# One core of Trainium2: loads reordered in the projections, a third gate buffer in the mixer, the last stage inside the experts' block

## The chip, the cores and the metric

One core of a Trainium2 chip runs one encoder layer in float32. The metric is the device time of one launch in microseconds (us); lower is better. The engines are TensorE (PE, matmuls), VectorE (DVE), ScalarE (ACT), GpSimd (POOL) and SyncE (SP, here only an issuer of DMAs); ACT and POOL issue DMAs as well. Each engine runs its own instructions in order, and waits on semaphores that others raise.

## The reference, cut to what matters

`x` is 512 prompt and 2048 sample tokens of width 1024, in two groups with their own conditioning.

```python
ada = silu(c) @ w_ada + b_ada;  sh1, sc1, gt1, sh2, sc2, gt2 = split(ada, 6)
h = rms_norm(x, norm_pre_mix) * (1 + sc1) + sh1
x = x + gt1 * rms_norm(token_mixer(h), norm_post_mix)
h = rms_norm(x, norm_pre_ffn) * (1 + sc2) + sh2
y = expert_choice_ffn(h)          # 16 experts, each takes its top tokens; y is a scatter-add
out = x + gt2 * rms_norm(y, norm_post_ffn)

# token_mixer: one projection h @ w_in feeds windowed attention and gated linear attention
merged = sigmoid(ga) * (attn @ w_branch_attn) + sigmoid(gg) * (o_g @ w_branch_gla)
return merged @ w_out
```

## The kernel before

Every float32 product is three matmuls of fp32r parts (`product3`, L108 to L112: hi by hi, lo by hi, hi by lo). ACT casts each operand to its hi part and DVE subtracts to get the lo part, so each weight chunk costs ACT a cast and DVE a `tensor_tensor`. The phases run one after the other, each in a block of its own. A block ends with a drain of every engine and a barrier: nothing of the next begins before the slowest engine has drained.

**Projections and attention** (`phase_proj_attn`, L416, about 45 to 845 us of the span). Five blocks of 512 tokens, in each 24 units (`BLOCK_UNITS`, L365), a unit being one 512-column slice of the projection. Block b also makes the normed and transposed `h` of block b+1: its four x tiles are loaded by SP (`load_x`, L529) into two buffers, ACT sums their squares (`squares`, L664) after units 1, 4, 10 and 14, POOL makes the reciprocal root (`rms`), DVE scales (`norm_x`, L809), PE turns the tile (L1022), ACT and DVE evict it, and POOL stores it to `scratch_hT` (`store_h`, L894). A buffer is free for its next x tile when that store has landed (`s_hst`). SP's queue is written by hand: in the loop over chunks c = 3 to 10, `load_w` for chunk c waits for the weight split of an earlier chunk, and tiles 2 and 3 of the block's four are loaded after the weights of c = 7 and c = 9 (L556). ACT begins the phase with nine small DMAs (L685 to L690), then splits the first weights and the first `h`; it ends that opening with a copy of `wa2` that waits for the nine (L694, L695). The gate `la` of the linear attention is read from its PSUM bank by ACT at L644, put through a softplus (L717), and bounded by DVE at L839.

**Gated linear attention** (`phase_gla`, L1100) to about 1541 us.

**The mixer** (`phase_mix`, L1826, about 1541 to 2104 us). Five blocks b of 512 tokens, in each 12 weight chunks m: eight branch chunks (both branch products of 128 channels) and four out chunks. For a branch chunk SP loads the two gate factors (`load_gate`, L1942, 512 KB), ACT takes their sigmoid in place (`gate`, L2029), DVE multiplies both with PE's result (L2126) and adds (L2128), ACT casts the sum to `m_hi` (L2068), and DVE subtracts to `m_lo` (`keep_lo`, L2132). There are two such gate buffers `sg`; the load for chunk m+1 waits until `keep_lo` of chunk m-1 has counted (`s_mlo`). During branch chunks, DVE, ACT, POOL and PE also finish the four token tiles of the block before: rms, gate row, residual x, second rms, PE's turn of the tile and the router's logits (L2288 to L2299, with evictions at L2062 and L2163). In block 0 SP also loads broadcast rows of `ada`, the bias and the norm weights (`load_rows`, at m = 1 for the mixer's gate and at m = 3 for the experts' gate); POOL makes from them two rows of each gate with eight 128x1024 `tensor_tensor` (L2246, L2249). The second pair is stored to `scratch_gate2` at m = 8, which ACT's first eviction of an out chunk waits for (`s_g2`). The last block's four `xn` tiles are stored by POOL (L2239).

**Routing** (`phase_route`, L2356) to about 2178 us, mostly a search for thresholds between DVE and PE.

**Experts** (`phase_experts`, L2575, 2178 to about 3646 us). For each of 16 experts POOL gathers token rows and scatters results; SP streams weights of 1 MB per chunk, ACT casts, DVE subtracts (L2716, L2768), PE multiplies. SP loads the experts' gate rows from `scratch_gate2` during expert 0 (L2660).

**Last stage** (`phase_final`, L2938, in a block of its own). Twenty tiles of 128 tokens: SP loads y (eight buffers), ACT sums squares and issues the stores three tiles behind (L2966, L2971), POOL makes the reciprocal root one tile at a time (L2983, L2985), DVE scales with the gate row and adds x (L2994, L2997) into one of six output buffers. SP waits for the last scatters before the first y load.

Of the kernel before, what the change touches and what calls it, by code (L numbers as in the profile page):

```python
# [8 lines left out]
F32 = mybir.dt.float32  # L9
# [406 lines left out]
def phase_proj_attn(nc, K, I, S):  # L416
# [10 lines left out]
    with Mem(nc, "pa") as M:  # L427
# [94 lines left out]
        with nc.Block() as block:  # L522
            @block.sync
            def _(sp):
# [20 lines left out]
                for b in range(NB):  # L545
# [25 lines left out]
            def _(act):  # L571
# [109 lines left out]

                act.wait_ge(s_z, 1)
# [8 lines left out]
                split_w(0)  # L691
                split_h(0, range(KD))
                split_w(1)
                act.wait_ge(s_c, 144)  # L694
                act.copy(wa2[:], wa_raw).then_inc(s_wa, 1)  # L695
                for b in range(NB):
                    for j, (kind, i, c) in enumerate(BLOCK_UNITS):
# [25 lines left out]
                        if b == NB - 1 and j in ADA:  # L723
                            read_ada(ADA[j])

# [1100 lines left out]
def phase_mix(nc, K, I, S):  # L1826
# [4 lines left out]
    with Mem(nc, "mix") as M:  # L1831
# [25 lines left out]
        s_g, s_sg = [M.sem(f"gate_loaded{i}") for i in range(2)], M.sem("gate")  # L1857
# [8 lines left out]
        s_row, s_add, s_gate, s_g2 = M.sem("rows_spread"), M.sem("gate_biased"), M.sem("gate_made"), M.sem("gate2_stored")  # L1866
# [30 lines left out]
        def x_of(b, t):  # L1897

            if b == LAST and t >= 2:
                return K.h_raw[:, 2 if t == 2 else 0].rearrange("p c n -> p (c n)")  # L1900
            return x[:, t % 2]
# [25 lines left out]
        with nc.Block() as block:  # L1927
            @block.sync
            def _(sp):
# [11 lines left out]
                def load_gate(b, c):  # L1941
                    g = b * KD + c  # L1942
                    if g >= NB * KD:
                        return
                    wait(sp, s_mlo, g - 1)
                    sp.dma_start(sg[:, g % 2], S["gate"][2 * c:2 * c + 2, :, b * BLK:(b + 1) * BLK].rearrange("c p n -> p c n"))\
                        .then_inc(s_g[g % 2], 16)

                def load_x(b, t):
# [3 lines left out]
                    elif t == 3:  # L1953
# [17 lines left out]
                load_gate(0, 1)  # L1971
                sp.dma_start(wr, I["w_router"][0].rearrange("(k p) n -> p k n", p=P)).then_inc(s_c, 16)
                def load_rows(n):
                    gate, beside = (K.gate1, x) if n == 0 else (mix, mix[:, 2:4])
                    at = (2 + 3 * n) * D
                    for g in range(2):
                        sp.dma_start(gate[:, g], S["ada"][g:g + 1, 3 * n * D:(3 * n + 1) * D].broadcast_to([P, D])).then_inc(s_row, 16)
                    sp.dma_start(beside[:, 0], I["b_ada"][:, at:at + D].broadcast_to([P, D])).then_inc(s_row, 16)
                    sp.dma_start(beside[:, 1], I[("norm_post_mix", "norm_post_ffn")[n]].broadcast_to([P, D])).then_inc(s_row, 16)

                for b in range(NB):
                    for m in range(NM):
                        load_w(b * NM + m + 3)
                        if b == 0 and m in (1, 3):
                            load_rows(m // 2)
                        if b == 0 and m == 8:
                            sp.wait_ge(s_gate, 4)
                            sp.dma_start(S["gate2"], mix[:, 0:2].rearrange("p g d -> p (g d)")).then_inc(s_g2, 16)
                        if b and m in (2, 4):
                            load_x(b - 1, (m + 2) // 2)  # L1990
                        if 1 <= m < 7:
                            load_gate(b, m + 1)
# [3 lines left out]
                    load_gate(b + 1, 1)  # L1996
                    load_x(b, 0)
# [3 lines left out]
                for t in range(TPB):  # L2001
                    n = LAST * TPB + t
                    sp.wait_ge(s_x1, n + 1)
                    sp.dma_start(S["x1"][n * P:(n + 1) * P, :], mix[:, t]).then_inc(s_last, 16)

            @block.scalar
            def _(act):
# [17 lines left out]
                def gate(g):  # L2025
                    if g >= NB * KD:
                        return
                    act.wait_ge(s_g[g % 2], 16 * (g // 2 + 1))
                    act.activation(sg[:, g % 2], sg[:, g % 2], ACT.Sigmoid).then_inc(s_sg, 1)  # L2029

                def evict(b, n, t):
                    u = b * NUB + 16 + 4 * n + t
                    act.wait_ge(s_u, u + 1)
                    if n == 0 and t == 0:
                        if b == 0:
                            act.wait_ge(s_g2, 16)
# [27 lines left out]
                def keep_hi(g):  # L2064
# [3 lines left out]
                    act.copy(m_hi[:, g % KD], sg[:, g % 2, 0]).then_inc(s_mhi, 1)  # L2068
# [982 lines left out]
```

## Time and profile before

| what | us |
|---|---|
| median of 3 runs (3712.59 to 3720.0) | 3719.83 |
| profiled execution | 3716.01 |
| its span, first to last instruction | 3714.3 |
| PE busy in the span | 3367.5 (91%) |
| DVE, ACT, POOL busy | 2195.5, 1609.1, 768.3 |
| mean granted TensorE clock | 0.955 of 2.4 GHz |

A row of the profile names the line, the engine, the operation and the operands; after the bar stand busy time, mean duration in ns, and idle time ahead with what ended it. In a table of waits the columns are: engine, line and operand that waited, what released it, then total us, number of waits, and the longest. A window row gives busy us of each engine with its instruction count, the granted clock (1.00 is 2.4 GHz and 0.50 is 1.2 GHz), the mean busy share of the 16 DMA engines, and GB/s.

### The profile page before, as it was taken

The page shows a single profiled execution, that of the slowest core. Times are in us where ns is not written, and L with a number is a line of the kernel's source. Part 1 is how long each engine was busy: PE and PEld are TensorE (multiplying, and loading weights), DVE is VectorE, ACT ScalarE, POOL GpSimd, SP SyncE. Part 2 cuts the span into 40 slices and gives each one's busy share as a digit, 9 for nine tenths or more (in the row PEclk, how much of TensorE's full clock was granted, in tenths as well). Part 3 has the DMA queues.
Part 4 walks back from the last instruction along what each step waited for, and adds up shares of the span by engine and source line. Part 5 has one row for each costly group of instructions (what it writes and reads, how often), then busy time and mean ns, then how long its engine had stood idle before and what let it go on. Part 6 is the DMA issues. An engine that isn't in the chain of part 4 may idle for free. (4 is left out here: it accounts for less than half of the span.)

```text
span 3714.3 us, 58093 instructions
## 1 busy us (share of the span) xinstructions
PE 3367.5 (91%) x21824; PEld 2852.1 (77%) x21824; DVE 2195.5 (59%) x4005; ACT 1609.1 (43%) x2478; POOL 768.3 (21%) x855
## 2 busy tenths in 40 slices
PE   6998999998899999889999549999999999999991
PEld 4777777676677777677777449999999999999991
DVE  3555455554588888555555465655555555555655
ACT  3666565553344444334444214444444444444442
POOL 1111111341134343223333201111111111111106
PEclk8999999998999999989999769999999999999995
DMA  6434344555645454556656325555555555555576
GB/s 218 162 124 147 136 130 148 161 196 162 197 149 167 133 172 130 151 193 224 222 193 218 157 88 183 164 174 174 170 174 164 170 169 168 171 164 173 166 263 240
DMA packets 540148, 637.28 MB, mean 172 GB/s; under 512 B 82528, under 2 KB 420544, under 8 KB 539712
## 3 DMA queue, kind: packets, MB, share of 16 engines
q1 hardware_dynamic: 491184, 485.78, 40.9%
q0 software_dynamic: 41920, 138.48, 11.8%
q10 hardware_dynamic: 6864, 10.60, 0.8%
q8 instruction: 115, 1.88, 0.2%
q14 instruction: 65, 0.53, 0.0%
HBM read 507.86 MB, written 126.91 MB: 171 GB/s over the span
## 5 line engine op out<-in xcount | busy, mean ns | idle before, releaser
L2768 DVE TENSOR_TENSOR moe_w_lo<-c_w_raw,moe_w_hi 128x2048 fp32r<-128x2048 f32 x192 | 439.8, 2291 | 368.6 <-ACT moe_w_hi L2716 368.6
L110 PE MATMUL moe_pg<-c_x_hi,moe_w_hi 128*128 128x320 f32 x2048 | 634.4, 310 | 1.8 <-DVE c_x_lo L2806 1.8
L112 PE MATMUL moe_pg<-c_x_hi,moe_w_lo 128*128 128x320 f32 x2048 | 632.8, 309 | 0.0
L111 PE MATMUL moe_pg<-c_x_lo,moe_w_hi 128*128 128x320 f32 x2048 | 632.8, 309 | 0.0
L2716 ACT CAST moe_w_hi<-c_w_raw 128x2048 fp32r<-128x2048 f32 x192 | 364.1, 1896 | 147.2 <-DMA c_w_raw<-in_w_gate_e_dram 74.2
L110 PEld LDWEIGHTS moe_pg<-c_x_hi,moe_w_hi 128*128 128x128 f32 x2048 | 384.4, 188 | 3.0 <-issue 2.2
L111 PEld LDWEIGHTS moe_pg<-c_x_lo,moe_w_hi 128*128 128x128 f32 x2048 | 384.5, 188 | 0.6
L112 PEld LDWEIGHTS moe_pg<-c_x_hi,moe_w_lo 128*128 128x128 f32 x2048 | 384.4, 188 | 0.0
L110 PE MATMUL gla_pd<-gla_h_hi,gla_w_hi 128*128 128x512 f32 x640 | 261.7, 409 | 26.3 <-DVE gla_h_lo L1228 23.8
L2690 POOL DMA_INDIRECT scratch_y<-moe_ys,moe_isc x48 | 83.1, 1730 | 825.9 <-ACT moe_ys L2757 699.2
L112 PE MATMUL gla_pd<-gla_h_hi,gla_w_lo 128*128 128x512 f32 x640 | 253.2, 396 | 0.0
L111 PE MATMUL gla_pd<-gla_h_lo,gla_w_hi 128*128 128x512 f32 x640 | 252.9, 395 | 0.0
L110 PE MATMUL pa_pu<-pa_h_hi,pa_w_hi 128*128 128x512 f32 x560 | 224.9, 402 | 18.2 <-DVE pa_h_lo L739 18.2
L111 PE MATMUL pa_pu<-pa_h_lo,pa_w_hi 128*128 128x512 f32 x560 | 219.5, 392 | 0.0
L112 PE MATMUL pa_pu<-pa_h_hi,pa_w_lo 128*128 128x512 f32 x560 | 219.4, 392 | 0.0
L1212 DVE TENSOR_TENSOR gla_w_lo<-c_w_raw,gla_w_hi 128x1024 fp32r<-128x1024 f32 x80 | 158.5, 1982 | 85.1 <-ACT gla_w_hi L1206 85.0
L110 PE MATMUL moe_pd<-moe_w_hi,moe_h_hi 128*128 128x512 f32 x512 | 204.4, 399 | 4.0 <-DVE moe_w_lo L2768 4.0
L111 PE MATMUL moe_pd<-moe_w_lo,moe_h_hi 128*128 128x512 f32 x512 | 199.9, 390 | 0.0
L112 PE MATMUL moe_pd<-moe_w_hi,moe_h_lo 128*128 128x512 f32 x512 | 199.8, 390 | 0.0
L2746 ACT CAST moe_h_hi<-moe_hd 128x320 fp32r<-128x320 f32 x128 | 58.9, 460 | 312.6 <-DVE moe_hd L2834 312.6
L110 PEld LDWEIGHTS gla_pd<-gla_h_hi,gla_w_hi 128*128 128x128 f32 x640 | 122.8, 192 | 56.3 <-DVE gla_w_lo L1212 18.8
L732 DVE TENSOR_TENSOR pa_w_lo<-c_w_raw,pa_w_hi 128x2048 fp32r<-128x2048 f32 x45 | 105.6, 2346 | 98.6 <-ACT pa_w_hi L577 98.5
(381 smaller groups left out, 7469.6 us busy)
## 6 DMA issues: line engine op xcount, KB each, us to landing
c_w_raw<-in_w_gate_e_dram SPq DMA_DIRECT2D x64, 1024.0 KB, 4.8
c_w_raw<-in_w_up_e_dram SPq DMA_DIRECT2D x64, 1024.0 KB, 4.8
c_w_raw<-in_w_down_e_dram SPq DMA_DIRECT2D x64, 1024.0 KB, 5.0
c_w_raw<-in_w_in_dram SPq DMA_DIRECT2D x80, 512.0 KB, 3.9
c_w_raw<-in_w_in_dram SPq DMA_DIRECT2D x35, 1024.0 KB
scratch_gate<-gla_sg POOLq DMA_DIRECT2D x80, 256.0 KB, 2.4
mix_sg<-scratch_gate SPq DMA_DIRECT2D x40, 512.0 KB, 5.6
c_h_raw<-scratch_hT SPq DMA_DIRECT2D x37, 512.0 KB, 6.6
```

Of the source, the lines that this page charges most:

```text
L110: pe.matmul(out, w_hi, x_hi, start=start, stop=False)
L111: pe.matmul(out, w_hi, x_lo, start=False, stop=False)
L112: return pe.matmul(out, w_lo, x_hi, start=False, stop=stop)
L732: dve.tensor_tensor(low, w_raw[:, m % 2, :, 0:n], w_hi[:, m % 2, :, 0:n].bitcast(F32), ALU.subtract).then_inc(s_wlo, 1)
L1212: dve.tensor_tensor(w_lo[:, n % WB], w_raw[:, n % 2], w_hi[:, n % WB].bitcast(F32), ALU.subtract).then_inc(d_wlo, 1)
L2690: pool.indirect_dma_start(out=S["y"], out_offset=bass.IndirectOffsetOnAxis(ap=isc[0:ROWS[r], r:r + 1], axis=0), in_=ys[0:ROWS[r], r], in_o ...
L2716: act.copy(w_hi[:, m % 2], w_raw[:, m % 2]).then_inc(s_whi, 1)
L2746: act.copy(h_hi[:, m // 2 * 2 + i, 0:CAP], hd[:, i]).then_inc(s_hhi, 1)
L2768: dve.tensor_tensor(w_lo[:, m % 2], w_raw[:, m % 2], w_hi[:, m % 2].bitcast(F32), ALU.subtract).then_inc(s_wlo, 1)
```

## The change

- Projections: ACT splits the first weights and `h` ahead of the nine small DMAs; the `wa2` copy with its wait is moved behind unit 1 of block 0. On SP's queue x tiles 2 and 3 of a block are loaded after the weights of c = 5 and 7 instead of 7 and 9.
- Mixer: three gate buffers, and the load for chunk m+2 instead of m+1 is issued at the same place; the residual x tiles take one buffer of their own and one in `K.h_raw[:, 2]`. Rows for the mixer's gate are loaded at m = 8 of block 0; the experts' gate is no longer made here, nor stored.
- The last block's four `xn` stores go from POOL to the end of SP's queue, with a semaphore of their own that POOL's first gather waits for.
- Experts: during expert 0 SP loads four broadcast rows (512 KB each) into `gate1` and two tiles of `K.x1`, and POOL makes the experts' gate with four `tensor_tensor` behind its first scatter.
- Last stage: moved to the end of the experts' block. y tiles lie in `w_hi` and `w_lo`, output tiles in `w_raw` and `ys`. POOL's reciprocal roots are made in seven batches. ACT issues stores six tiles behind.

```diff
-                        if c in (7, 9) and b < NB - 1:
-                            load_x(4 * b + (c - 3) // 2)
+                        if c in (5, 7) and b < NB - 1:
+                            load_x(4 * b + (c - 1) // 2)
...
+                split_w(0)
+                split_h(0, range(KD))
                 act.wait_ge(s_z, 1)
                 for n in range(3):
...
-                split_w(0)
-                split_h(0, range(KD))
                 split_w(1)
-                act.wait_ge(s_c, 144)
-                act.copy(wa2[:], wa_raw).then_inc(s_wa, 1)
...
+                        if b == 0 and j == 1:
+                            act.wait_ge(s_c, 144)
+                            act.copy(wa2[:], wa_raw).then_inc(s_wa, 1)
...
-        sg = M.sb("sg", [P, 2, 2, BLK])
+        sg = M.sb("sg", [P, 3, 2, BLK])
-        x = M.sb("x", [P, 2, D])
+        x = M.sb("x", [P, D])
...
-                    wait(sp, s_mlo, g - 1)
-                    sp.dma_start(sg[:, g % 2], ...)
+                    wait(sp, s_mlo, g - 2)
+                    sp.dma_start(sg[:, g % 3], ...)
...
-                        if b == 0 and m in (1, 3):
-                            load_rows(m // 2)
                         if b == 0 and m == 8:
-                            sp.wait_ge(s_gate, 4)
-                            sp.dma_start(S["gate2"], mix[:, 0:2].rearrange("p g d -> p (g d)")).then_inc(s_g2, 16)
+                            load_rows()
...
-                        if 1 <= m < 7:
-                            load_gate(b, m + 1)
+                        if 1 <= m < 6:
+                            load_gate(b, m + 2)
...
+                for t in range(TPB):
+                    n = LAST * TPB + t
+                    sp.wait_ge(s_xn, n + 1)
+                    sp.dma_start(S["xn"][n * P:(n + 1) * P, :], xn_of(LAST, t)).then_inc(K.last_xn_stored, 16)
...
-                for t in range(TPB):
-                    store_xn(LAST, t)
...
-                        sp.dma_start(K.gate1[:].rearrange("p g d -> p (g d)"), S["gate2"]).then_inc(K.s_gate2, 16)
+                        for g in range(2):
+                            sp.dma_start(K.gate1[:, g], S["ada"][g:g + 1, 3 * D:4 * D].broadcast_to([P, D])).then_inc(s_rows, 16)
+                        sp.dma_start(K.x1[:, 0], I["b_ada"][:, 5 * D:6 * D].broadcast_to([P, D])).then_inc(s_rows, 16)
+                        sp.dma_start(K.x1[:, 1], I["norm_post_ffn"].broadcast_to([P, D])).then_inc(s_rows, 16)
...
+                    if is_exp(e, 0):
+                        pool.wait_ge(s_rows, 64)
+                        for g in range(2):
+                            pool.tensor_tensor(K.gate1[:, g], K.gate1[:, g], K.x1[:, 0], ALU.add).then_inc(s_gadd, 1)
+                        for g in range(2):
+                            pool.wait_ge(s_gadd, g + 1)
+                            pool.tensor_tensor(K.gate1[:, g], K.gate1[:, g], K.x1[:, 1], ALU.mult).then_inc(s_gate2, 1)
                 peeled(pool, N_EXP, body)
+                for i, (a, z) in enumerate(BATCHES):   # (0,1) (1,2) (2,4) (4,8) (8,12) (12,16) (16,20)
+                    pool.wait_ge(s_q, z)
+                    pool.tensor_scalar(rs_fin[:, a:z], ss[:, a:z], 1.0 / D, EPS, ALU.mult, ALU.add).then_inc(s_v, 1)
+                    pool.wait_ge(s_v, i + 1)
+                    pool.tensor_tensor(rs_fin[:, a:z], rs_fin[:, a:z], K.neghalf[:, 0:z - a], ALU.pow).then_inc(s_r, 1)
...
+                    act.activation(junk_tile(n), y_tile(n), ACT.Square, accum_out=ss[:, n:n + 1]).then_inc(s_q, 1)
+                    if n >= 6:
+                        store(n - 6)
```

## Rows read from the trace of the kernel before

**Rows 1.** Waits of PE: engine, line, releaser, then total us, times, longest.

```profile
PE pa_pu L1022 <- DVE pa_st L839: 24.8, 4, 7.2
PE pa_pu L110 <- DVE pa_h_lo L739: 18.2, 5, 11.6
PE mix_p_r L2288 <- DVE c_logit L2159: 18.2, 8, 3.5
PE mix_p_r L2299 <- DVE mix_xT L2163: 9.9, 1, 9.9
PE mix_pu L110 <- DVE mix_w_lo L2112: 3.7, 1, 3.7
```

**Rows 2.** Waits of ACT, the same columns.

```profile
ACT mix_sg L2029 <- DMA mix_sg<-scratch_gate: 120.6, 30, 8.8
ACT pa_row L664 <- DMA pa_x<-in_x_sample_dram: 31.2, 4, 8.7
```

**Rows 3.** Windows: us from the span's start, length, busy by engine, clock, DMA.

```profile
136.70:143.50 6.80, 5.16 (x23) 4.76 (x24) 4.75 (x15) 6.74 (x10) 1.53 (x3) 0.50 0.11 41
...
594.10:600.90 6.80, 4.90 (x21) 4.50 (x22) 4.53 (x14) 6.74 (x10) 1.72 (x4) 0.50 0.09 39
...
1597.60:1614.70 17.10, 9.21 (x30) 7.98 (x31) 13.99 (x13) 5.26 (x7) 7.19 (x3) 0.50 0.53 184
...
1666.00:1725.00 59.00, 52.28 (x280) 42.16 (x279) 42.03 (x48) 29.23 (x39) 27.75 (x26) 0.97 0.72 241
...
1976.00:2036.00 60.00, 54.80 (x283) 43.94 (x282) 42.65 (x49) 29.23 (x39) 28.44 (x26) 0.94 0.74 250
...
1550.00:1563.00 13.00, 9.89 (x34) 7.41 (x35) 5.30 (x5) 7.11 (x7) 0.00 (x0) 0.88 0.90 255
3652.00:3690.00 38.00, 0.00 (x0) 0.00 (x0) 32.26 (x26) 16.78 (x30) 34.72 (x26) 0.50 1.01 399
...
3646.50:3714.30 67.80, 0.00 (x0) 0.00 (x0) 50.17 (x40) 22.99 (x40) 53.06 (x40) 0.50 0.79 310
```

**Rows 4.** Timeline of ACT, 127 to 138 us: start, duration, instruction, idle ahead.

```profile
134.94 0.63 ACT L664 ACTIVATE pa_row<-pa_x 128x512 bf16<-128x512 f32 x1 [7.49 <-DMA pa_x<-in_x_sample_dram]
```

**Rows 5.** Timeline of SP's queue, 84 to 132 us: start, duration to the last issue.

```profile
96.04 7.81 SPq L150 DMA_DIRECT2D c_w_raw<-in_w_in_dram  x2
...
129.03 0.56 SPq L531 DMA_DIRECT2D pa_x<-in_x_sample_dram  x1
```

**Rows 6.** Timeline of POOL, 76 to 105 us: the store of an h tile.

```profile
83.33 1.13 POOL L894 DMA_DIRECT2D scratch_hT<-pa_x  x1 [0.54 <-ACT pa_x L672]
```

**Rows 7.** Timeline of ACT, 44 to 64 us: first weight cast of the projections.

```profile
49.86 1.90 ACT L577 CAST pa_w_hi<-c_w_raw 128x2048 fp32r<-128x2048 f32 x1 [6.71 <-issue]
```

**Rows 8.** Timeline of DVE, 1573 to 1606 us: the same operation twice.

```profile
1579.38 3.35 DVE L2112 TENSOR_TENSOR mix_w_lo<-c_w_raw,mix_w_hi 128x1024 fp32r<-128x1024 f32 x1
...
1587.16 1.23 DVE L2112 TENSOR_TENSOR mix_w_lo<-mix_w_third,mix_w_hi 128x1024 fp32r<-128x1024 f32 x1 [0.25 <-ACT mix_w_hi L2017]
```

**Rows 9.** Timeline of POOL, 1573 to 1606 us: the last two of eight gate operations.

```profile
1598.71 6.08 POOL L2249 TENSOR_TENSOR mix_mix<-mix_mix 128x1024 f32<-128x1024 f32 x2
```

**Rows 10.** Timeline of ACT, 1690 to 1705 us: sigmoid of one branch chunk.

```profile
1702.91 1.06 ACT L2029 ACTIVATE mix_sg<-mix_sg 128x1024 f32<-128x1024 f32 x1 [3.88 <-DMA mix_sg<-scratch_gate]
```

**Rows 11.** Drain of POOL at the end of the mixer: count, ns min/median/max, first and last start.

```profile
L1927 POOLq DRAIN  x1: 4447/4447/4447, 2099.3 to 2099.3; - x1
```

**Rows 12.** Drain of POOL at the end of the experts, same columns.

```profile
L2623 POOLq DRAIN  x1: 9573/9573/9573, 3636.8 to 3636.8; - x1
```

**Rows 13.** Groups by line, 3646 to 3714 us: busy us, mean ns, idle before.

```profile
L2985 POOL TENSOR_TENSOR fin_r<-fin_r,c_neghalf 128x1 f32<-128x1 f32 x20 | 29.7, 1484 | 1.7
L2994 DVE SCALAR_TENSOR_TENSOR fin_o<-fin_y,fin_r,c_gate 128x1024 f32<-128x1024 f32 x20 | 25.7, 1284 | 24.8 <-POOL fin_r L2985 24.8
L2983 POOL TENSOR_SCALAR fin_r<-fin_ss 128x1 f32<-128x1 f32 x20 | 23.4, 1169 | 15.4 <-ACT fin_junk L2971 14.0
```

**Rows 14.** Timeline of DVE, 2290 to 2300 us: a weight split of the experts.

```profile
2294.47 2.29 DVE L2768 TENSOR_TENSOR moe_w_lo<-c_w_raw,moe_w_hi 128x2048 fp32r<-128x2048 f32 x1 [2.91 <-ACT moe_w_hi L2716]
```

More of the change, by code:

```diff
@@ L1856, in phase_mix @@
         s_w, s_whi, s_wlo = K.mix_w + [M.sem("w_loaded2")], M.sem("w_hi"), M.sem("w_lo")
-        s_g, s_sg = [M.sem(f"gate_loaded{i}") for i in range(2)], M.sem("gate")
+        s_g, s_sg = [M.sem(f"gate_loaded{i}") for i in range(3)], M.sem("gate")
         s_half, s_u, s_ra, s_rd = M.sem("half_done"), M.sem("unit_done"), M.sem("unit_read_act"), M.sem("unit_read_dve")
@@ L1996, in _ @@
                     load_gate(b + 1, 1)
+                    load_gate(b + 1, 2)
                     load_x(b, 0)
@@ L2067, in keep_hi @@
                         wait(act, s_u, g // KD * NUB)
-                    act.copy(m_hi[:, g % KD], sg[:, g % 2, 0]).then_inc(s_mhi, 1)
+                    act.copy(m_hi[:, g % KD], sg[:, g % 3, 0]).then_inc(s_mhi, 1)
                 split(0)
@@ L2241, in _ @@
                 clear_spent(pool, K)
[L2242 to L2249 removed]
+                pool.wait_ge(s_row, 64)
+                for g in range(2):
+                    pool.tensor_tensor(K.gate1[:, g], K.gate1[:, g], x[:], ALU.add).then_inc(s_add, 1)
+                for g in range(2):
+                    pool.wait_ge(s_add, g + 1)
+                    pool.tensor_tensor(K.gate1[:, g], K.gate1[:, g], K.h_raw[:, 2].rearrange("p c n -> p (c n)"), ALU.mult)\
+                        .then_inc(s_gate, 1)
                 for b in range(LAST):
@@ L2607, in phase_experts, with tile_of, y_tile, o_tile @@
         s_rest = M.sem("unused_rows_zero")
+        s_rows, s_gadd, s_gate2 = M.sem("gate2_rows"), M.sem("gate2_biased"), M.sem("gate2_made")
+        NY, NO = 8, 6
+        NP = N_PROMPT // P
+        ORDER = list(range(NP, NT)) + list(range(NP))
+        BATCHES = [(0, 1), (1, 2), (2, 4), (4, 8), (8, 12), (12, 16), (16, 20)]
+        ss, rs_fin = M.sb("ss", [P, NT]), M.sb("rs_fin", [P, NT])
+        s_st = [M.sem(f"stored{i}") for i in range(NO)]
+        s_q, s_v, s_r, s_m, s_o = M.sem("squares"), M.sem("mean"), M.sem("rstd"), M.sem("normed"), M.sem("made")
+        s_y = [M.sem(f"y_loaded{i}") for i in range(NY)]
+        def tile_of(buffers, i):
+            flat = buffers[i // 4].rearrange("p a n -> p (a n)")
+            return flat[:, i % 4 * D:(i % 4 + 1) * D]
+        def y_tile(n):
+            return tile_of((w_hi[:].bitcast(F32), w_lo[:].bitcast(F32)), n % NY)
+        def o_tile(n):
+            i = n % NO
+            return K.w_raw[:, i // 2, i % 2 * D:(i % 2 + 1) * D] if i < 4 else ys[:, i - 4]
+        def junk_tile(n):
+            return oh[:, n % 4 * 4:n % 4 * 4 + 4].rearrange("p t n -> p (t n)")
         s_yl, s_yp = M.sem("prompt_low"), M.sem("prompt_sum")
@@ L2762, in _, with store @@
                 peeled(act, N_EXP, body)
+                def store(n):
+                    t = ORDER[n]
+                    dst = outs[0][0, t * P:(t + 1) * P, :] if t < NP else outs[1][0, (t - NP) * P:(t - NP + 1) * P, :]
+                    act.wait_ge(s_o, n + 1)
+                    act.dma_start(dst, o_tile(n)).then_inc(s_st[n % NO], 16)
+                for n in range(NT):
+                    act.wait_ge(s_y[n % NY], 16 * (n // NY + 1))
+                    wait(act, s_q, n - 3)
+                    act.activation(junk_tile(n), y_tile(n), ACT.Square, accum_out=ss[:, n:n + 1]).then_inc(s_q, 1)
+                    if n >= 6:
+                        store(n - 6)
+                for n in range(NT - 6, NT):
+                    store(n)
+                for i in range(NO):
+                    act.wait_ge(s_st[i], 16 * len(range(i, NT, NO)))
             @block.vector
@@ L2856, in _ @@
                 peeled(dve, N_EXP, body)
+                dve.wait_ge(s_gate2, 2)
+                dve.wait_ge(K.s_x1, 16 * NT)
+                for n, t in enumerate(ORDER):
+                    dve.wait_ge(s_r, [i for i, (a, z) in enumerate(BATCHES) if a <= n < z][0] + 1)
+                    wait(dve, s_st[n % NO], 16 * (n // NO))
+                    dve.scalar_tensor_tensor(out=o_tile(n), in0=y_tile(n), scalar=rs_fin[:, n:n + 1],
+                                             in1=K.gate1[:, 0 if t < NP else 1], op0=ALU.mult, op1=ALU.mult).then_inc(s_m, 1)
+                    dve.wait_ge(s_m, n + 1)
+                    dve.tensor_tensor(o_tile(n), o_tile(n), kept_x1(K, t), ALU.add).then_inc(s_o, 1)
             @block.tensor
```

123 lines of the change are left out of this document (34 added, 89 removed).

## The prediction

> **What bounds the kernel now.** I read first the busy shares (PE works 91% of the span), then the waits of PE: what the change can win is PE's idle time, the stretches behind it in which PE runs at 1.2 instead of 2.4 GHz, and the last stage, where PE has nothing to do. The experts, 40% of the span, keep PE fed, so nothing is to be had there. The reader should see in PE's waits [rows 1] four turns of x tiles in the projections (24.8 us in all), one opening wait (11.6), the logits in the mixer (18.2 in one of its lines) and two single waits of 9.9 and 3.7 in the mixer's first block; in ACT's waits [rows 2] the same things from the other side: 31.2 us for x tiles, 120.6 for gate factors. The windows [rows 3] show what a stretch is limited by: a turn's stretch at clock 0.50, a branch stage of the mixer with PE busy 52 of 59 us and no engine full, a last stage without PE. Timelines then tell who was late.
>
> **Projections, x tiles.** ACT sits 7.49 us at the squares of x tile 3 and starts them at 134.94 [rows 4]; that load was issued at 129.03 [rows 5], because on SP's queue it stands behind two weight loads that wait for buffers. Behind the squares stands ACT's read of a gate bank, then DVE's L839, then PE's turn. The same four times: 31.2 us for ACT [rows 2], 24.8 for PE [rows 1]. The change puts both x loads one buffer turn earlier. Tile 3 then goes out about where tile 2 does now, 25 us earlier than today, against 5.9 us that its landing took: the wait goes. Cover: the store that frees the buffer is issued at 83.33 [rows 6] and by my estimate takes about what the x load took, 5.9 us; tile 2's load can thus go at 89, while the next weight load goes at 96.04 [rows 5], so SP has 7 us in hand. Next late is ACT's own work: the squares take two halves of 0.63, so the gate bank is read when PE arrives, or up to 1 us after. Behind each gap PE ran at 0.50; first and last of the four stretches show 5.16 and 4.90 us of matmuls [rows 3], so four of them hold some 20, and 10 come back at full clock. Together 24.8 + 10 = 35 at best; without the clock 25. I take 33.
>
> **Projections, opening.** Nine DMA issues stand ahead of the first cast at 49.86, with 6.71 us of idle by "issue" [rows 7]. In front of them the casts start some 4 us earlier, under an 11.6 us wait of PE [rows 1]. But the nine now stand ahead of the second weight split, so the second chunk comes hardly earlier, and the first turn still waits for tables. Between 0 and 4, I take 1.7. The `wa2` copy is one small operation, behind unit 1 no later needed than before, and the nine transfers have landed by then: nothing.
>
> **Mixer, first block.** POOL's last two gate operations run from 1598.71 for 6.08 us [rows 9], and beside such ones DVE's L2112 took 3.35 us, against 1.23 alone [rows 8]. PE waits 3.7 for it and 9.9 for an eviction queued behind it [rows 1], and runs 9.21 us of matmuls at 0.50 [rows 3]. At m = 8 the row loads and the four remaining operations lie in the out stage, where DVE has no weight deadline as close (PE's out chunk has twice the matmuls). 3.7 + 9.9 + 9.2/2 = 18; without the clock 13.6. I take 18. DVE's first gate scaling comes in the next block, a stage later.
>
> **Mixer, blocks 1 to 4.** A gate load is issued when `keep_lo` of the chunk before last has counted, and ACT's sigmoid waits 3.88 us for it [rows 10], thirty times, 120.6 us [rows 2]. It sets DVE's cycle, and behind DVE stand the logits (18.2 us of PE [rows 1]). With a third buffer the load has a whole chunk (59/8 = 7.4 us) more, and the sigmoid finds its data. Then DVE (42 us of 59) and PE (52.3) remain [rows 3]: PE sets the stage. The four windows are 59 to 60 us with PE busy 52.28 in the first and 54.80 in the last [rows 3], so 6.7 and 5.2 us of idle, some 25 in all, and clocks of 0.97 and 0.94 that hold back some 5 more: 30 at best. Some idle stays, since PE has to turn tiles between logits that DVE feeds. Low end 8: as much as if only the clock dips and a few waits went. I take 22, nearer to the idle that the rows show.
>
> **xn stores.** POOL's drain lasts 4.45 us behind its last store [rows 11], and the other engines had finished; SP's queue issues the stores instead. I take 4 (0 to 4.4: at nothing if SP's drain waits as POOL's does). The Trainium skill, "DMA: Bandwidth & Descriptors", section "Issuing engines are not separate DMA queues", says that DMAs of any issuer run on the same 16 engines and that spreading saves only issue time; by that the stores take as long and the sum would be 4 less. The row is about the issuer's drain, on which the page says nothing.
>
> **Last stage.** POOL's drain begins at 3636.8 and takes 9.57 us [rows 12], so the first y load goes at 3646.5; without a block's end it goes when the scatters have landed, 4 to 5.5 us earlier by estimate. Then POOL's pair, 1.48 + 1.17 = 2.65 a tile [rows 13] with its handoffs, paces DVE, whose own two operations fill 50.2 of 67.8 us [rows 3]. Seven batches take POOL off the chain: up to 8 us. Next late are the transfers: share 1.01 at 399 GB/s in the thick of it, mean 0.79 over 67.8 us, which is 53.6 us of full share [rows 3]. So the stage can't shrink below some 56, and the gain is 14 at most. A batch of four also waits for its last tile. 4 if only the start is won. I take 10. The same page, section "Where 436 GB/s comes from", has some 358 GB/s as what HBM gives a core; 20 loads and 20 stores of 512 KB, 21 MB, would be an estimated 59 us, and the gain some 7. The trace has 399 over 38 us, against it.
>
> **Experts' gate, the cost.** Four 512 KB loads take the place of one of 1 MB, and four 128x1024 operations run on POOL beside DVE, 11 us by [rows 9]. DVE's 2.29 us split at 2294.47 [rows 14] is stretched as in [rows 8], 3.35/1.23 = 2.7 times, by 3.9 us. PE's next chunk needs it at once, and a clock that falls would be on top. Between 0 (POOL's operations fall between DVE's) and 6 (two splits in part); I take 3, nearer to one split's stretch. SP's new wait for the gate stands in the last expert, more than a millisecond behind: nothing.
>
> **Sum.** 33 + 1.7 + 18 + 22 + 4 + 10 − 3 = 86; against the profiled 3716 us, 3630. That execution lies 4 below the median of the three, within their spread.
>
> **Rivals.**
> (a) Transfers bound the mixer's branch stage. It moves 241 GB/s at a share of 0.72; a stretch with the same narrow packets shows 255 at 0.90 [rows 3], so some 283 at full share, and 14.2 MB in 50 us: just below the 52 of PE. For it: the loads then crowd. Against: it needs all of PE's idle gone. Mixer gain 8, time 3644.
> (b) The clock stays: PE still pauses a little at each turn, and the halves (10 + 4.6 us) don't come back: 3645. For it: the clock fell after gaps smaller than these too (0.97 and 0.94 in the branch stages). Against: the stretches lie right behind the long waits.
> (c) The last stage stays bound by transfers or the batches' waits: gain 4, 3636; by the page's 358 GB/s 7, 3633.
> (d) The xn stores' landing is waited for on SP as on POOL, which is where the page's rule would lead: 3634.
> (e) The change doesn't do what it says: ACT still waits for x tiles, because the earlier load waits for the h store behind which POOL is late. 33 lost, 3663.
> (f) The other side: SP's queue is in order. If the h store of tile 0 lands after 96 us [rows 5, 6], the weight loads behind the x load come late, and PE with them. It decides from 7 us of lateness; each us beyond costs about one in each of four blocks. To eat 86 us it must be some 22 us beyond, 29 late; at 25 beyond, 3716 + 14 = 3730. The store's issue is fixed by ACT's and DVE's evictions, so this needs a queue that I misread.
>
> **Chances.** Forecast, 3618 to 3641, with (c) and (d) inside it by size: 0.66 (0.06 of it (c) by its own reasons, 0.02 the page's 358, 0.03 (d)). Better than 3618: 0.08. (a) 0.10, (b) 0.08, (e) 0.05, (f) 0.03. Range: 3610 takes the upper ends of all terms (35 + 4 + 18 + 30 + 4.4 + 14, no cost: 105); 3650 holds (a) or (b) with a few us lost elsewhere; it leaves out (e), (f) and (a) with (b). A measurement of this kernel tells 0.2%, 7.4 us, from no change; every case but (f) is beyond it. Faster 0.95, same 0.02, slower 0.03.
>
> **What would show it.** Right: no PE wait at L1022 and no clock of 0.50 behind the four turns; the first mixer block without the 9.9 us wait, its branch stage some 18 us shorter; branch stages of 53 to 55 us with ACT's gate wait near nothing; no 4 us POOL drain before routing; y loads from about 3642 less the rest, and DVE back to back. Wrong: ACT's gate wait remains (a), PE's idle gone but 0.50 still there (b), DVE pausing every fourth tile at the end (c), a new wait of SP at the x loads with PE idle for weights (f), a wait of PE in the second expert over 6 us.

## The result

The changed kernel takes 3629.86 us, median of four runs (3627.0 to 3631.08), the kernel before 3718.02 us (now four runs, 3712.59 to 3720.0); the ratio is 0.9764, interval 0.9747 to 0.9781. The profiled execution has a span of 3629.0 us at a mean clock of 0.964. The forecast was 3630.0. The total hits, but errors of opposite sign cancel in it, as the terms below show.

TensorE runs the same 21824 matmuls in the same order in both kernels, so the start of one and the same matmul can be compared in the two traces. The gain grows and shrinks like this:

| the same point of the work | before, us | after, us | difference | this step | forecast of the step |
|---|---|---|---|---|---|
| first turn of an x tile | 79.15 | 76.73 | -2.4 | opening -2.4 | -1.7 |
| projections, behind the fourth late turn | 700.36 | 661.62 | -38.7 | x tiles -36.3 | -33 |
| mixer, before the gate rows of before | 1559.27 | 1521.36 | -37.9 | +0.8 | 0 |
| mixer, behind them | 1615.57 | 1557.69 | -57.9 | first block -20.0 | -18 |
| mixer, last turns | 2089.15 | 2008.42 | -80.7 | blocks 1 to 4 -22.9 | -22 |
| routing, first product | 2109.26 | 2024.31 | -85.0 | xn stores -4.2 | -4 |
| second expert, before its second chunk | 2295.29 | 2211.94 | -83.3 | +1.6 | 0 |
| a chunk later | 2304.09 | 2232.38 | -71.7 | experts' gate +11.6 | +3 |
| last matmul | 3633.71 | 3562.08 | -71.6 | 0 | 0 |
| end of the span | 3714.3 | 3629.0 | -85.3 | last stage -13.7 | -10 |

The page of the kernel after shows PE's share and its clock in 40 slices: the low slices, in the routing (2019 to 2092 us) and in the last stage, are what is left.

```profile
PE 3349.1 (92%) x21824; PEld 2839.7 (78%) x21824; DVE 2200.8 (61%) x4005; ACT 1608.5 (44%) x2478; POOL 734.5 (20%) x825
...
PEclk9999999999999999999999589999999999999996
```

PE's waits of the kernel after (line, releaser, total us, times, longest), to be held against [rows 1]:

```profile
PE pa_pu L110 <- DVE pa_h_lo L740: 13.6, 5, 6.6
...
PE moe_pg L110 <- DVE moe_w_lo L2831: 8.9, 1, 8.9
...
PE mix_p_r L2287 <- DVE c_logit L2161: 7.1, 9, 1.5
...
PE pa_pu L1023 <- DVE pa_x L803: 1.3, 1, 1.3
```

The four turns (24.8 us) have no row any longer, the logits went from 18.2 to 7.1 us, the single waits of 9.9 and 3.7 us are gone. A row is new: PE waited 8.9 us once for a weight split of DVE in the experts. ACT's rows for x tiles and for gate factors [rows 2] are both gone.

Windows of the kernel after, columns as in [rows 3]: the branch stages that answer to 1666 and 1976 us of before, a stretch behind a turn, the first block's branch stage, the stretch behind the new wait, and the thick of the last stage.

```profile
1608.00:1660.60 52.60, 50.57 (x278) 40.87 (x276) 40.84 (x46) 29.18 (x39) 26.84 (x24) 1.00 0.77 259
1900.70:1954.10 53.40, 51.03 (x282) 41.33 (x281) 41.50 (x47) 29.18 (x39) 27.56 (x25) 1.00 0.78 266
128.00:134.80 6.80, 6.80 (x58) 6.56 (x57) 4.99 (x15) 6.67 (x12) 0.79 (x1) 1.00 0.49 175
1521.40:1557.70 36.30, 36.30 (x177) 30.52 (x176) 27.29 (x39) 19.10 (x22) 0.00 (x0) 1.00 0.79 240
2222.70:2226.80 4.10, 4.06 (x15) 4.06 (x16) 4.10 (x12) 0.00 (x0) 0.01 (x1) 0.50 0.73 251
3571.00:3610.00 39.00, 0.00 (x0) 0.00 (x0) 32.99 (x28) 21.39 (x37) 13.91 (x12) 0.50 1.02 410
```

Behind a turn PE is now busy all of 6.8 us at full clock, where it had 5.16 us at 0.50. The branch stages take 52.6 and 53.4 us instead of 59 and 60, with PE busy 96%. The new wait, like the old ones, is followed by a stretch at 0.50.

Where the new wait comes from stands in the timelines of DVE and POOL from 2205 to 2235 us of the kernel after (start, duration, instruction; L2742 and L2745 are the experts' gate).

```profile
2211.12 11.57 DVE L2831 TENSOR_TENSOR moe_w_lo<-c_w_raw,moe_w_hi 128x2048 fp32r<-128x2048 f32 x1 [2.91 <-ACT moe_w_hi L2762]
...
2224.37 2.28 DVE L2831 TENSOR_TENSOR moe_w_lo<-c_w_raw,moe_w_hi 128x2048 fp32r<-128x2048 f32 x1
```

```profile
2210.71 5.24 POOL L2742 TENSOR_TENSOR c_gate<-c_gate,c_x 128x1024 f32<-128x1024 f32 x2
2215.41 5.12 POOL L2745 TENSOR_TENSOR c_gate<-c_gate,c_x 128x1024 f32<-128x1024 f32 x2
```

DVE's split takes 11.57 us where [rows 14] has 2.29: it was issued 0.4 us behind POOL's first operation and ends 2.2 us behind POOL's last. It wasn't slowed, it stood still for all four.

The last stage by line (busy us, mean ns, idle ahead) and POOL's drain at the end of the mixer, for [rows 13] and [rows 11]:

```profile
L2751 POOL TENSOR_TENSOR moe_rs_fin<-moe_rs_fin,c_neghalf 128x4 f32<-128x4 f32 (+2 forms) x7 | 11.5, 1644 | 0.6
L2925 DVE SCALAR_TENSOR_TENSOR c_w_raw<-moe_w_hi,moe_rs_fin,c_gate 128x1024 f32<-128x1024 f32 x8 | 10.2, 1280 | 12.7 <-POOL moe_rs_fin L2751 12.7
```

```profile
L1929 POOLq DRAIN  x1: 3279/3279/3279, 2012.4 to 2012.4; - x1
...
L1929 SPq DRAIN  x1: 122/122/122, 2018.7 to 2018.7; - x1
```

POOL's seven batches no longer hold DVE: of 12.7 us of idle 11.6 lie ahead of the first tile. POOL's drain now begins at 2012.4, under the mixer's last work, and SP's takes 0.12 us. SP's first y load stands 7.4 us behind the last matmul (3569.5 against 3562.1), where it stood 12.9 us behind it.

### The profile page after: what moved, and what is told of

It reads as the page before. It is cut to its first block and busy times, and to the rows that moved or that the text cites. A ratio compares the mean times of both kernels' runs of the same rounds, so it can differ in the third digit from the quotient of the medians.

```text
span 3629.0 us, 58054 instructions
## 1 busy us (share of the span) xinstructions
PE 3349.1 (92%) x21824; PEld 2839.7 (78%) x21824; DVE 2200.8 (61%) x4005; ACT 1608.5 (44%) x2478; POOL 734.5 (20%) x825
## 5 line engine op out<-in xcount | busy, mean ns | idle before, releaser
L2831 DVE TENSOR_TENSOR moe_w_lo<-c_w_raw,moe_w_hi 128x2048 fp32r<-128x2048 f32 x192 | 449.0, 2339 | 369.1 <-ACT moe_w_hi L2762 369.1
```

Source lines behind the costliest of these rows:

```text
L2831: dve.tensor_tensor(w_lo[:, m % 2], w_raw[:, m % 2], w_hi[:, m % 2].bitcast(F32), ALU.subtract).then_inc(s_wlo, 1)
```

## The experiments

Theory: each term is what its step said, and the new wait is POOL's gate operations shutting DVE out. Each run below changes the changed kernel in one thing, unless it says otherwise. All but one are single executions, to be read against 3627 to 3631 us; the kernel before, run beside them on three occasions, took 3717.85 (seven runs, 3712.51 to 3731.46), 3721.73 and 3718.27 us, so a total alone can be some us off. Sizes therefore come from the start of the same matmul in the two traces, which drifts by 1 to 6 us over the projections and the linear attention without a cause here.

**No gate operations.** The four operations are taken out of POOL's body.

```diff
-                            pool.tensor_tensor(K.gate1[:, g], K.gate1[:, g], K.x1[:, 0], ALU.add).then_inc(s_gadd, 1)
...
-                            pool.tensor_tensor(K.gate1[:, g], K.gate1[:, g], K.x1[:, 1], ALU.mult).then_inc(s_gate2, 1)
...
```

> The changed kernel without POOL's four gate operations in the experts; the row loads and the waits stay, so the experts' gate factor is raw and the output is left incomplete in that. Theory 1 (POOL's operations shut DVE out of its weight split): DVE's split at that place takes 2.3 instead of 11.57 us, PE's 8.9 us wait there goes, the clock stays at 2.4 GHz, and the time falls by some 12 us, to about 3618. Theory 2 (the 2 MB of row loads delay the weights): the wait stays, 3630.

3618.5 us. DVE's split takes 2.29 us, PE has no wait there, and PE gains 11.6 us there on the kernel after. The row loads cost nothing: theory 2 falls.

**One gate operation.**

```diff
-                        for g in range(2):
-                            pool.tensor_tensor(K.gate1[:, g], K.gate1[:, g], K.x1[:, 0], ALU.add).then_inc(s_gadd, 1)
+                        pool.tensor_tensor(K.gate1[:, 0], K.gate1[:, 0], K.x1[:, 0], ALU.add).then_inc(s_gadd, 1)
...
```

> Only the first of POOL's four gate operations is left in the experts (the other three are left out, so the gate is incomplete). If one operation of POOL holds DVE's split up until it ends, the split takes some 2.3 + 2.0 = 4.3 us, PE waits about 1.7 us, and the cost is 2 to 3 us: 3620. If the 11.57 us were a slower rate of DVE beside POOL (2.7 times, as the first block of the mixer before suggests), the split takes some 4 us too, but its end then doesn't follow POOL's end. If the long split has another cause than POOL's operations, it stays at 11.6 us, and the time at 3630.

3620.87 us. DVE and POOL in its timeline:

```profile
2210.53 4.68 DVE L2827 TENSOR_TENSOR moe_w_lo<-c_w_raw,moe_w_hi 128x2048 fp32r<-128x2048 f32 x1 [2.91 <-ACT moe_w_hi L2758]
```

```profile
2210.12 2.93 POOL L2741 TENSOR_TENSOR c_gate<-c_gate,c_x 128x1024 f32<-128x1024 f32 x1
```

4.68 - 2.29 = 2.4 us of standing still, and PE waits 2.0. This is the size that the prediction had counted for all four.

**Sixteen small gate operations.**

```diff
-                            pool.tensor_tensor(K.gate1[:, g], K.gate1[:, g], K.x1[:, 0], ALU.add).then_inc(s_gadd, 1)
+                        for q in range(8):
+                            at = slice(q % 4 * 256, q % 4 * 256 + 256)
+                            pool.tensor_tensor(K.gate1[:, q // 4, at], K.gate1[:, q // 4, at], K.x1[:, 0, at], ALU.add).then_inc(s_gadd, 1)
...
```

> The same gate work on POOL at the same place, in sixteen operations of 256 columns instead of four of 1024. Theory 1a (DVE gets in as soon as the running POOL operation ends): the split waits 0.7 us and takes 3.0 us, POOL's operations wait for it in turn, PE waits about 0.5 us, 3618. Theory 1b (a row of POOL operations without a pause keeps DVE out until the last ends): the split takes over 11 us again and the time is 3630 or a little more.

3626.86 us, in a trace that already stood 5.6 us earlier than the changed kernel's ahead of that place; across it PE loses 0.9 us more than there, so the cost is no smaller. Theory 1b holds: sixteen operations in a row, and DVE got in between none of them.

```profile
2205.54 13.17 DVE L2833 TENSOR_TENSOR moe_w_lo<-c_w_raw,moe_w_hi 128x2048 fp32r<-128x2048 f32 x1 [2.91 <-ACT moe_w_hi L2764]
```

```profile
2205.13 6.03 POOL L2743 TENSOR_TENSOR c_gate<-c_gate,c_x 128x256 f32<-128x256 f32 x8
2210.64 5.91 POOL L2747 TENSOR_TENSOR c_gate<-c_gate,c_x 128x256 f32<-128x256 f32 x8
```

PE's wait was 10.5 us.

**Halved splits on DVE.**

```diff
-                    dve.tensor_tensor(w_lo[:, m % 2], w_raw[:, m % 2], w_hi[:, m % 2].bitcast(F32),
-                                      ALU.subtract).then_inc(s_wlo, 1)
+                    for half in range(2):
+                        at = slice(half * (WCH // 2), (half + 1) * (WCH // 2))
+                        ins = dve.tensor_tensor(w_lo[:, m % 2, at], w_raw[:, m % 2, at], w_hi[:, m % 2, at].bitcast(F32), ALU.subtract)
+                    ins.then_inc(s_wlo, 1)
```

> The changed kernel with every weight split of the experts on DVE in two operations of 1024 columns instead of one of 2048. In the mixer DVE's operations of 512 and 1024 columns did get in between two POOL operations, in the experts the one of 2048 did not. If the width of DVE's operation decides, the first half gets in after POOL's first operation and the second after its second: the split ends some 5 us later than alone, PE waits some 3 to 4 us instead of 8.9, and the time is some 3623. If the place or the row of POOL operations decides, PE waits 8.9 us as before and the time is 3630. DVE has room for the extra operations: no other rise.

3630.04 us. The width of DVE's operation doesn't decide: two halves took 11.63 us together, and PE waited 8.9 again.

```profile
2209.21 11.63 DVE L2833 TENSOR_TENSOR moe_w_lo<-c_w_raw,moe_w_hi 128x1024 fp32r<-128x1024 f32 x2 [2.91 <-ACT moe_w_hi L2762]
```

**Gate operations one by one, each behind a split.**

```diff
+                        for k in range(4):
+                            pool.wait_ge(s_wlo, NM + 2 + k)
...
```

> The changed kernel with POOL's four gate operations one by one, each released by the end of a weight split on DVE (the second to fifth of the second expert), so that each runs while DVE waits for ACT's next cast. Theory (a POOL operation costs only where it meets a split): no split is longer than some 3 us, PE has no wait there, and the time is 3618. If even a single operation beside the other work of DVE costs PE time, it is 3620 to 3628.

3619.2 us. No split is longer than 2.29 us and PE has no wait. What POOL met instead were DVE's one-hot operations: ten of them took 4.01 us beside it, 1.84 alone, in DVE's slack.

```profile
2213.19 2.41 POOL L2745 TENSOR_TENSOR c_gate<-c_gate,c_x 128x1024 f32<-128x1024 f32 x1 [2.36 <-DVE moe_w_lo L2834]
2219.24 2.42 POOL L2745 TENSOR_TENSOR c_gate<-c_gate,c_x 128x1024 f32<-128x1024 f32 x1 [3.64 <-DVE moe_w_lo L2834]
```

```profile
2212.95 4.01 DVE L2842 TENSOR_SCALAR moe_oh<-c_place,c_pos 128x64 bf16<-128x64 bf16 x10
2216.89 2.28 DVE L2834 TENSOR_TENSOR moe_w_lo<-c_w_raw,moe_w_hi 128x2048 fp32r<-128x2048 f32 x1
```

**Gate made by DVE behind the last expert.** A version to keep. ACT's squares of the last stage now wait for the gate as well.

```diff
-                            pool.tensor_tensor(K.gate1[:, g], K.gate1[:, g], K.x1[:, 0], ALU.add).then_inc(s_gadd, 1)
...
+                        if is_exp(e, N_EXP - 1) and 5 <= m < 9:      # SP: one of the four rows per chunk
...
+                act.wait_ge(s_gate2, 2)
...
                 peeled(dve, N_EXP, body)
+                dve.wait_ge(s_rows, 64)
+                for g in range(2):
+                    dve.tensor_tensor(K.gate1[:, g], K.gate1[:, g], row_tile(0), ALU.add).then_inc(s_gadd, 1)
...
+                    dve.tensor_tensor(K.gate1[:, g], K.gate1[:, g], row_tile(1), ALU.mult).then_inc(s_gate2, 1)
```

> The experts' gate is made by DVE behind the last expert, where it waits 11.65 us for the first reciprocal root; the four rows are loaded one by one in the last expert (chunks 5 to 8), bias and norm weights into the one-hot buffer that is free by then. Four operations of 1.22 us take 4.9 of the 11.65 us, so the last stage begins when it did. Theory 1: the 12 us in the second expert are gone and nothing takes their place: 3617, some 2.7% under the kernel before. Rival: the rows' 2 MB in the last expert delay its weights, or the squares of ACT, which now wait for the gate, start later: then it is 3618 to 3625.

3617.01 us, median of four (3616.62 to 3618.5); ratio to the kernel before 0.9719, interval 0.9696 to 0.9741. This is 12.85 us below the changed kernel's median, 11.7 of it in the second expert. The four operations fill 4.6 us of a wait that DVE has anyway, and 8.29 us of it are left:

```profile
3548.02 2.35 DVE L2917 TENSOR_TENSOR c_gate<-c_gate,moe_oh 128x1024 f32<-128x1024 f32 x2
3550.30 2.35 DVE L2920 TENSOR_TENSOR c_gate<-c_gate,moe_oh 128x1024 f32<-128x1024 f32 x2
3560.93 1.28 DVE L2926 SCALAR_TENSOR_TENSOR c_w_raw<-moe_w_hi,moe_rs_fin,c_gate 128x1024 f32<-128x1024 f32 x1 [8.29 <-POOL moe_rs_fin L2745]
```

**x loads late again.**

```diff
-                        if c in (5, 7) and b < NB - 1:
-                            load_x(4 * b + (c - 1) // 2)
+                        if c in (7, 9) and b < NB - 1:
+                            load_x(4 * b + (c - 3) // 2)
```

> The changed kernel with x tiles 2 and 3 loaded after the weights of c = 7 and 9 again, nothing else. Theory (the x loads alone made the turns wait): four waits of PE at the turn come back, 5.7 to 7.2 us each, with stretches at 1.2 GHz behind them; the time rises by 33 to 37 us, to 3663 to 3667. Rival (the clock would stay low anyway, or another part made the gain): a rise of 25 or less.

3668.51 us, a rise of 38.7, above the 33 to 37 that I had expected. The turns wait again, and behind the fourth of them PE stands 39 us later. The two rows that name the cause come back as they were [rows 1, 2]:

```profile
PE pa_pu L1023 <- DVE pa_st L840: 24.9, 4, 7.1
```

```profile
ACT pa_row L664 <- DMA pa_x<-in_x_sample_dram: 31.2, 4, 8.6
```

**Gate load one chunk ahead.**

```diff
-                    wait(sp, s_mlo, g - 2)
+                    wait(sp, s_mlo, g - 1)
...
-                load_gate(0, 2)
...
-                        if 1 <= m < 6:
-                            load_gate(b, m + 2)
+                        if 1 <= m < 7:
+                            load_gate(b, m + 1)
...
-                    load_gate(b + 1, 2)
```

> The changed kernel with the load for chunk m+1 instead of m+2 at the same place in the queue, so the third gate buffer is not used ahead. Theory (ACT's wait for gate factors sets the branch stage): ACT waits some 120 us for gate factors again, the branch stages of blocks 1 to 4 take 59 us, and the time rises by some 24 us, to 3654. Rival (the transfers or the other edits in the mixer set the stage): 3632 to 3640.

3655.07 us, a rise of 25.2; in the trace some 26 us gather from the second block's branch stage to the last's, and none in the first block. ACT's waits and the window of the second block's branch stage:

```profile
ACT mix_sg L2031 <- DMA mix_sg<-scratch_gate: 104.0, 30, 6.1
```

```profile
1608.50:1667.80 59.30, 52.40 (x280) 42.23 (x279) 42.20 (x48) 29.30 (x39) 27.83 (x26) 0.97 0.71 239
```

**Gate rows early in the mixer.** Loaded at m = 1 of block 0, bias and norm rows into `mix`.

```diff
-                        if b == 0 and m == 8:
+                        if b == 0 and m == 1:
                             load_rows()
...
+                        if b == 0:
+                            act.wait_ge(s_gate, 2)
```

> The changed kernel with the mixer's gate rows loaded at m = 1 of block 0 (beside rows into the mix buffer) instead of m = 8: four of the eight POOL operations of before are back in the branch stage. By the lock of theory 1 DVE's evictions in that stretch wait for POOL and PE waits 3.7 us once, with 1.7 us more of low clock: some 5 us, 3635. If it were the second set of rows, or all 3 MB of loads, that mattered: under 2 us.

3631.23 us; in block 0 PE loses 2.5 us (from 1.4 ahead of the changed kernel to 1.1 behind it), not the 5 that I had expected, and not the under 2 of the rival. DVE's operations were held as before:

```profile
1541.33 3.43 DVE L2116 TENSOR_TENSOR mix_w_lo<-mix_w_third,mix_w_hi 128x1024 fp32r<-128x1024 f32 x1
```

```profile
1534.68 6.17 POOL L2248 TENSOR_TENSOR c_gate<-c_gate,mix_mix 128x1024 f32<-128x1024 f32 x2 [29.23 <-DMA mix_mix<-in_norm_post_mix_dram]
1540.80 6.22 POOL L2251 TENSOR_TENSOR c_gate<-c_gate,mix_mix 128x1024 f32<-128x1024 f32 x2
```

**Both: rows early, gate load one chunk ahead.**

> Both edits of the two earlier runs together: rows at m = 1 of block 0, and the gate load only one chunk ahead. Alone the rows cost 2 us and the gate load nothing in block 0. If POOL's lock on DVE alone made the first block's waits, block 0 loses 2 us again, and the time is 3656. If the waits came of both (the row loads delay the gate load, and two buffers don't cover it), block 0 loses 5 us or more: ACT waits 6 to 9 us once for gate factors there, and the time is 3659 or more.

3657.82 us. In block 0 PE loses 6.1 us (from 1.9 us ahead of the changed kernel to 4.1 behind it), two and a half times what the rows cost alone, and the wait of ACT is there:

```profile
1535.94 1.06 ACT L2031 ACTIVATE mix_sg<-mix_sg 128x1024 f32<-128x1024 f32 x1 [8.65 <-DMA mix_sg<-scratch_gate]
```

```profile
PE mix_pu L110 <- DVE mix_w_lo L2114: 3.0, 1, 3.0
```

So the first of the two waits in the first block (3.7 us of PE [rows 1]) came of two things together: row loads that delay a gate load with no chunk in hand, and POOL's operations that hold DVE when it wants to make up for it. The second (9.9 us) did not come back: no run put the second set of rows and its four operations back.

**Single reciprocal roots in the last stage.**

```diff
-        BATCHES = [(0, 1), (1, 2), (2, 4), (4, 8), (8, 12), (12, 16), (16, 20)]
+        BATCHES = [(n, n + 1) for n in range(20)]
```

> The changed kernel with POOL's reciprocal roots tile by tile in the last stage, as before, but inside the experts' block. Theory (POOL's pair of 2.65 us and its handoffs set the pace): DVE takes a tile each 2.98 us instead of 2.46, so the stage grows by some 8 to 9 us, to 3638. Rival (transfers set it): under 3 us.

3635.23 us. The last matmul came 4.5 us earlier than in the changed kernel's trace and the end 4.4 us later, so the stage is 8.9 us longer. That is the batches' share; the other 13.7 - 8.9 = 4.8 us I put down to the block's end with its drain. No run undid that alone, but the first y load agrees: it stands 5.4 us nearer to the last matmul than before.

```profile
L2751 POOL TENSOR_TENSOR moe_rs_fin<-moe_rs_fin,c_neghalf 128x1 f32<-128x1 f32 x20 | 29.7, 1484 | 1.7
```

**Opening and xn stores as before**, in one kernel.

```diff
-                split_w(0)
-                split_h(0, range(KD))
                 act.wait_ge(s_z, 1)
...
+                    pool.wait_ge(s_xn, n + 1)
+                    pool.dma_start(S["xn"][n * P:(n + 1) * P, :], xn_of(LAST, t)).then_inc(K.last_xn_stored, 16)
```

> Two undone edits far apart in time, read at PE's own instructions: the opening of the projections as before (nine small DMAs first, the wa2 copy ahead of the units), and the last block's xn stores on POOL's queue. Opening: PE's first product 4.4 us later, and 2.4 us of that left at the first turn of an x tile. xn stores: the first instruction of routing 4.2 us later, by POOL's drain. Time together 3636. Rival for the stores (their landing is waited for wherever they are issued): no rise there, 3632.

3639.39 us. PE's first product comes 5.0 us later and 3.7 of it are left at the first turn; routing begins another 4.2 us later, behind this drain:

```profile
L1928 SPq DRAIN  x1: 124/124/124, 2009.8 to 2009.8; - x1
...
L1928 POOLq DRAIN  x1: 4433/4433/4433, 2021.8 to 2021.8; - x1
```

The rival that SP would wait for the landing falls: in the kernel after, SP's drain takes 0.12 us, right behind the stores that it issued.

## Why the prediction was right, and where it wasn't

**x tiles: right.** The cause is shown by the run that undoes it alone: the same four waits and the low clock behind them come back. 36 to 39 us against 33, and against 35 at best: I left 2 us for a next wait of ACT that did not come, and the low clock held back some 11.5 us (36.3 - 24.8, with drift in it), not 10. SP's queue had the room that the step claimed (PE waited 0.2 us once for a weight split in the projections), so rival (f) did not begin.

**Opening: right in kind**, 2.4 us (3.7 where it was undone) against 1.7, within the bounds given.

**First block of the mixer: size right, cause half right, and shown for the smaller part.** 20.0 against 18. I put it down to POOL's operations beside DVE. PE lost the 20 us in two places: 5.7 behind the first four operations (the wait of 3.7), and 14.4 behind the second four (the wait of 9.9). The run with both edits brings the first place back, 6.1 us. It takes two things for that: with a third gate buffer the same operations cost 2.5 us, and the late gate load without the early rows costs nothing in this block. The half of the cause that the step left out is the gate load held up by the row loads, 8.65 us for ACT. The step had the row for it in [rows 2] (longest wait 8.8) and didn't use it here. The second place came back in no run. The rows of before show the same pair there, a late gate load ahead of held operations of DVE, the last of them the eviction that PE waits for:

```profile
1595.54 1.06 ACT L2029 ACTIVATE mix_sg<-mix_sg 128x1024 f32<-128x1024 f32 x1 [8.41 <-DMA mix_sg<-scratch_gate]
```

```profile
1599.23 3.35 DVE L2112 TENSOR_TENSOR mix_w_lo<-c_w_raw,mix_w_hi 128x1024 fp32r<-128x1024 f32 x1
...
1602.70 2.64 DVE L2163 COPY mix_xT<-c_b 128x1024 f32<-128x1024 f32 x1
```

So for 14.4 of the 20 us the cause is read from rows and not shown, and which of the edits took them away is open.

**Blocks 1 to 4: right, with two sizes off that cancel.** 22.9 against 22; undone alone it is 25 to 26. PE sets the branch stage now, busy 50.57 of 52.60 us. The step put the clock's part at some 5 us; clocks of 0.97 and 0.94 over 59 and 60 us hold back 1.8 and 3.6 us a stage, some 11 in four, and PE's busy time fell by 1.7 and 3.8 us. Idle gave less than its 25: of 6.7 and 5.2 us a stage 2.0 and 2.4 are left. Rival (a), the transfers, is refuted: they moved 259 and 266 GB/s at shares of 0.77 and 0.78.

**Clock, rival (b): refuted.** Where the waits left, the windows show 1.00.

**xn stores: right.** 4.2, and 4.2 again when undone. The Trainium skill, "DMA: Bandwidth & Descriptors", section "Issuing engines are not separate DMA queues", would have given nothing here, since the transfers share the same engines whoever issues them. The drain rows show why that doesn't carry over: what was saved is not transfer time but the drain that ends last, 4.43 us on POOL and 0.12 on SP. How much of the 4.43 is due to the stores is open: without them POOL's drain still takes 3.28 us, but it ends ahead of DVE's and SP's work.

**Last stage: mechanism right, sized low.** 13.7 against 10: batches 8.9 and, by difference, the block's end 4.8. I had taken off too much for the doubt that transfers would hold the stage (rival c): they moved 410 GB/s at a share of 1.02 over 39 us, and DVE still ran without a gap from its fourth tile on. The Trainium skill, "DMA: Bandwidth & Descriptors", section "Where 436 GB/s comes from", has some 358 GB/s for HBM to a core; it did not bind in this stage, where the trace has 410.

**Experts' gate: the step that failed.** The term was 3 us (0 to 6) and measured 11.6. The step took from [rows 8] a rate, 3.35 / 1.23 = 2.7 times slower, and applied it to one split of 2.29 us. POOL's row of the same moment shows something else:

```profile
1578.86 2.79 POOL L2249 TENSOR_TENSOR c_gate<-c_gate,mix_x 128x1024 f32<-128x1024 f32 x1
```

This operation ends at 1581.65, and DVE's split of [rows 8] at 1582.73, 1.1 us later, about the 1.23 that it takes alone: DVE stood still until POOL's running operation ended, and then ran at its own speed. With that reading the price depends on how long POOL goes on, not on how long the split is. The prediction's own sign of being wrong here, a wait of PE in the second expert over 6 us, came: 8.9. One operation costs 2.4 us of DVE and 2.0 of PE, four in a row 9.3 and 8.9, with a stretch at 0.50 behind. The Trainium skill, "SBUF — State Buffer", section "Who interferes with whom", states just this: a DVE instruction with two SBUF inputs and a POOL instruction that reads SBUF exclude each other for a whole instruction, and the second to issue blocks fully. The run with one operation agrees (4.68 us, of which 2.29 is the split). For four in a row it would let me expect one operation's length, some 2.4 us; the trace has 9.3.

**The total** came out within 1 us because the gains were each larger than forecast (0.7 + 3.3 + 2.0 + 0.9 + 0.2 + 3.7 = 10.8), and this cost, 8.6 us larger, and drifts of 2.4 us took as much back. That is luck of cancelling, not precision: the terms were good to 2 to 4 us each, and one was off by a factor of four.

## What to carry to other kernels

When an operation takes longer beside another engine's, don't read a rate out of it: look at whether it ends just its own time behind the other's end. If so, it waited, and its price is what is left of the other's operation (2.4 us for one here) or, as in the experts, of its whole run. Put such work where the blocked engine has nothing due: four operations in a row on POOL cost 11.6 us, next to nothing one by one behind a split, and nothing when DVE itself makes them in a wait at the end. A buffer more and a load elsewhere can be two cures of one wait; undo them singly and together before crediting either.

## What the runs showed that I had not expected

- POOL operations in a row kept DVE out altogether in the experts (four: 11.57 us; sixteen small ones: 13.17 us; with DVE's split halved: 11.63 us), while in the mixer DVE got in between two of them: L2112 took 3.35 us in [rows 8], L2116 3.43 in the run with early rows, with four POOL operations queued. The width of DVE's operation and the length of POOL's do not decide it alone; what does is open.
- DVE's one-hot operations, which have one SBUF tensor as input and a column as scalar, were held beside POOL too: ten took 4.01 instead of 1.84 us.
- A drain of POOL behind stores that it issued itself took 4.43 us, one of SP behind the same stores 0.12. In the kernel after, POOL's drain still ends the projections (6.58 us from 806.7) and the linear attention (4.05 us from 1504.0) as the last of its block; no run tried to move these.
- What made POOL's reciprocal roots slow in the last stage of before may be the same exclusion, with POOL as the one that waits. Its two operations on 128x1 take 0.19 and 0.57 us for the first tile, where DVE has no work yet, and 1.28 and 1.53 us beside DVE's operations of 1.2 to 1.3 us. The one of 1.28 ends at 3659.23, DVE's operation beside it at 3659.19. No run tested this reading; its rows are:

```profile
3650.96 0.19 POOL L2983 TENSOR_SCALAR fin_r<-fin_ss 128x1 f32<-128x1 f32 x1 [12.52 <-ACT fin_junk L2971]
3651.23 0.57 POOL L2985 TENSOR_TENSOR fin_r<-fin_r,c_neghalf 128x1 f32<-128x1 f32 x1
...
3657.95 1.28 POOL L2983 TENSOR_SCALAR fin_r<-fin_ss 128x1 f32<-128x1 f32 x1
3659.32 1.53 POOL L2985 TENSOR_TENSOR fin_r<-fin_r,c_neghalf 128x1 f32<-128x1 f32 x1
```
